# A stage function of its own for the banded attention of layer 0: two query tiles a step, the sink inside the minimum, four store buffers

## What is computed

```python
def swa_sink_attention(q, k, v, bias_table, sinks):      # 8 query heads, 2 key heads, HD = 64
    ...                                                  # each chunk of 64 sees itself and the chunk before
    s = jnp.einsum('bcqhgd,bckhd->bhgcqk', qc, kb) * ATTN_SCALE + bias
    s = jnp.where(valid[:, None, :], s, -jnp.inf)
    sink = jnp.broadcast_to(sinks..., s.shape[:-1] + (1,))
    p = jax.nn.softmax(jnp.concatenate([s, sink], axis=-1), axis=-1)[..., :WINDOW]
    o = jnp.einsum('bhgcqk,bckhd->bcqhgd', p, vb)
```

## Time and profile before

| | |
|---|---|
| median of 3 runs (2572.9 to 2577.78) | 2573.3 us |
| the profiled execution's own time | 2574.83 us |
| its span, first to last instruction | 2573.0 us |
| PE busy | 2390.8 us (93%) |
| DVE busy | 1524.9 us (59%) |
| ACT busy | 1139.8 us (44%) |
| POOL busy | 1072.9 us (42%) |
| stage B, first matmul to first matmul of the output stage | 977.91 to 1089.62 us |

### The profile page before, as it was taken

How to read it: one execution, slowest core, us unless ns; L and a number is a source line. 1 busy time by engine, 2 the same in 40 slices (tenths; PEclk the granted TensorE clock), 3 DMA queues, 4 the chain that set the end, 5 groups by cost and what they waited for, 6 DMA issues and landing times. The chain is left out here.

```text
span 2573.0 us, 46411 instructions
## 1 busy us (share of the span) xinstructions
PE 2390.8 (93%) x17864; PEld 1979.2 (77%) x17864; DVE 1524.9 (59%) x2879; ACT 1139.8 (44%) x2400; POOL 1072.9 (42%) x853
## 2 busy tenths in 40 slices
PE   5999999997999998899979999899997999998998
PEld 4777778875878877678767888788886888887887
DVE  6444665435898896756554423744223888887555
ACT  4333343333777776612133333433332666665221
POOL 6777768772000002211058877678874201100000
PEclk9999999997999999999989999999998999999999
DMA  3555434457565224657334444344433453443452
GB/s 129 174 172 176 153 124 156 142 170 161 119 144 111 62 96 140 176 190 279 130 123 164 164 115 143 112 156 160 143 99 121 156 193 133 161 157 112 160 201 82
DMA packets 220746, 376.77 MB, mean 146 GB/s; under 512 B 54980, under 2 KB 108912, under 8 KB 219504
## 3 DMA queue, kind: packets, MB, share of 16 engines
q1 hardware_dynamic: 199376, 296.21, 36.0%
q0 software_dynamic: 19792, 75.50, 9.9%
q10 hardware_dynamic: 1360, 2.10, 0.2%
HBM read 236.33 MB, written 142.90 MB: 147 GB/s over the span
## 5 line engine op out<-in xcount | busy, mean ns | idle before, releaser
L1092 PE MATMUL p_acc<-p_operands,p_w_hi 128*128 128x512 f32 x1600 | 612.0, 393 | 5.7 <-DVE p_full_out L959 5.5
L1092 PE MATMUL p_acc<-share,p_w_hi 128*128 128x512 f32 x1024 | 385.3, 397 | 12.0 <-DVE p_operands L735 5.7
L310 POOL TENSOR_TENSOR p_w_lo<-p_w_raw,p_w_hi 128x512 fp32r<-128x512 f32 x240 | 333.2, 1397 | 151.1 <-ACT p_w_hi L573 150.8
L1092 PEld LDWEIGHTS p_acc<-p_operands,p_w_hi 128*128 128x128 f32 x1600 | 302.7, 190 | 67.7 <-POOL p_w_raw L328 4.7
L1092 PE MATMUL p_acc<-share,p_w_lo 128*128 128x512 f32 x896 | 350.7, 391 | 0.0
L573 ACT ACTIVATE p_w_hi<-p_w_raw 128x512 fp32r<-128x512 f32 x252 | 156.6, 624 | 245.5 <-POOL p_w_raw L328 106.5
L1092 PE MATMUL p_acc<-share_low,p_w_hi 128*128 128x512 f32 x624 | 249.3, 400 | 12.0 <-DVE p_operands L735 6.1
L1092 PE MATMUL p_acc<-share_low,p_w_lo 128*128 128x512 f32 x624 | 245.2, 393 | 0.0
L1092 PEld LDWEIGHTS p_acc<-share,p_w_hi 128*128 128x128 f32 x1024 | 192.4, 189 | 54.0 <-DVE p_operands L735 8.5
L865 DVE SCALAR_TENSOR_TENSOR p_lo_out<-p_full_out,p_hi_out 128x512 fp32r<-128x512 f32 x116 | 122.6, 1057 | 182.5 <-ACT p_hi_out L590 182.5
L1898 DVE CUSTOM_DVE_ANT_0 c_prob<-c_logits,c_bias 128x640 f32<-128x640 f32 (+4 forms) x256 | 179.5, 739 | 65.6 <-PE c_logits L1812 49.5
(11 more groups left out here) (283 smaller groups left out, 4771.1 us busy)
## 6 DMA issues: line engine op xcount, KB each, us to landing
scr_qh<-p_hi_out SPq DMA_DIRECT2D x116, 256.0 KB, 2.5
scr_ql<-p_lo_out SPq DMA_DIRECT2D x116, 256.0 KB, 2.6
p_w_raw<-in_w_in_even POOLq DMA_DIRECT2D x26, 1024.0 KB, 7.5
scr_gt<-p_hi_out SPq DMA_DIRECT2D x128, 128.0 KB, 2.0
ready_w<-in_w_in_odd POOLq DMA_DIRECT2D x16, 1024.0 KB, 7.0
p_w_raw<-in_w_in_odd POOLq DMA_DIRECT2D x16, 1024.0 KB, 6.9
share<-scr_qh SPq DMA_DIRECT2D x28, 512.0 KB, 8.4
share<-scr_ql SPq DMA_DIRECT2D x28, 512.0 KB, 9.6
```

The source lines that it names most:

```text
L310: nc.gpsimd.tensor_tensor(w_lo[:, k, :, :], w_source(e, k), w_hi[:, k, :, :].bitcast(F32), ALU.subtract).then_inc(w_made, 1)
L1092: last = nc.tensor.matmul(bank[:, :], wt[:, k, c, :], at[k][:, c, :], start=starts and step == 0, stop=step == 3 * HK - 1, skip_group_chec ...
```

## The change

Stage B gets a function of its own, `small_attn`, and `band_attn` keeps only what stage C uses. What is different in stage B:

- A step is two query tiles of a pair of heads: 32 steps in place of 64. PE does 12 `qk` rows, 16 transposes and 16 `pv` rows a step; DVE four minima and one copy of both tiles (L2093; in a pair's first step, where 64 columns of each half are not written, two copies).
- The logits of a step take four PSUM banks of two sets; `turned` stays single, and holds both tiles.
- The sink is the starting value of the minimum, read from `keep["sink"]` for each partition. Logits and bias have 256 columns. The sink's share of the sums is added once at the end: a subtraction on DVE (L2101), an exponential on ACT (L2136), an addition on DVE.
- The column of zeros and its four memsets, and the wait of PE for them, are gone.
- There are four output buffers and four store semaphores, one for each quarter of the rows. The copy of a block waits for the store of the same quarter of the pair before. In the output stage `load_block(b)` waits for the stores of quarter b.

```diff
-        nc.gpsimd.tensor_copy(bias[:, :, NEAR], self.keep["sink"][:, :]).then_inc(masked, 1)
...
-        self.stored = [ctx.enter_context(nc.semaphore(f"{name}_stored{i}")) for i in range(2)]
+        self.stored = [ctx.enter_context(nc.semaphore(f"{name}_stored{i}")) for i in range(TILES // TPB)]
...
-                    act.wait_ge(stored[n % 2], 16 * (n // 2))
+                    act.wait_ge(stored[(n - 2) % STORES], 16 * ((n - 2) // STORES + 1))
...
+def small_attn(nc, before, keep, scr, w_dram, w_loaded, w_hi, w_lo, post, share, ready, ssq, rms):
...
+            def qk(n):
...
+                if n >= 2:
+                    pe.wait_ge(max_done, 2 * TWO * (n - 1))
+                for j, i in tiles_of(n):
...
+            def transposes(n):
+                if n >= 1:
+                    pe.wait_ge(copied, copies[n])
+                for j, i in tiles_of(n):
+                    for a in range(2):
+                        pe.wait_ge(exp_done, 2 * TWO * n + 2 * j + a + 1)
...
+            for n in range(N + 2):
+                if n < N:
+                    qk(n)
+                if 1 <= n <= N:
+                    transposes(n - 1)
+                if n >= 2:
+                    pv(n - 2)
...
+                        nc.vector.tensor_tensor_reduce(out=prob[:, n % 2, j, half, 0:cols], in0=logits[n % 2][half][:, (j + 1) * NEAR - cols:(j + 1) * NEAR],
+                                                       in1=bias[:, h, NEAR - cols:NEAR], scale=1.0, scalar=keep["sink"][:, h:h + 1],
+                                                       op0=ALU.add, op1=ALU.min, accum_out=neg_max[:, h, i:i + 1]).then_inc(max_done, 1)
...
+            for n in range(N + 1):
+                if n < N:
+                    maxima(n)
+                if n == N:
+                    dve.wait_ge(max_done, 2 * TWO * N)
+                    nc.vector.tensor_tensor(sink_exp[:, :, :], neg_max[:, :, :], keep["sink"][:, :].unsqueeze(2).to_broadcast([P, B_HEADS, TILES]), ALU.subtract).then_inc(sink_less, 1)
+                if n >= 1:
+                    leaves(n - 1)
+            dve.wait_ge(root_done, 1)
...
+            nc.vector.tensor_tensor(sums[:, :, :], sums[:, :, :], sink_exp[:, :, :], ALU.add).then_inc(summed, 1)
...
+            def output_leaves(g):
+                act.wait_ge(pv_done, 2 * (g + 1))
+                hp, r = divmod(g, STORES)
+                if hp >= 1:
+                    act.wait_ge(stored[r], 16 * hp)
+                nc.scalar.activation(o_out[:, r, :], o_ps[:, g % 2, :], ACT.Copy).then_inc(o_done, 1)
...
-                    sp.wait_ge(post.stored[1], 16 * post.heads)
+                sp.wait_ge(post.stored[b], 16 * (post.heads // 2))
```

More of the change, by code:

```diff
@@ L1597, in widen, with band_attn @@
                               self.inv_sums[:, :, t:t + 1].to_broadcast([P, self.heads, HD])).then_inc(self.widened, 1)
-def band_attn(nc, before, name, keep, scr, heads, back, q_row, k_row, group, v_dram, skew, o_row, sinks, w_dram, w_loaded, w_hi, w_lo, post, share, ready=None, ssq=None, rms=None, ahead=None):
+def band_attn(nc, before, name, keep, scr, heads, back, q_row, k_row, v_dram, skew, o_row, w_dram, w_loaded, w_hi, w_lo, post, share, ahead):
     with ExitStack() as ctx:
@@ L1696, in _ @@
         def _(sp):
[L1697 to L1704, removed]
+            for n in range(len(FIRST)):
+                first_piece(sp, n, 0)
+            for n in range(HALVES):
+                load_qk(sp, 1, n)
+                load_v(sp, 1, n)
             def store(hp, r):
@@ L1776, in _ @@
             for n in range(D // W_PART):
[L1777 removed]
+                if 2 <= n < HP:
                     load_bias(n)
@@ L1812, in qk @@
                             last = nc.tensor.matmul(logits[half][:, lo:hi], q_sb[b][x][rows, i * P:(i + 1) * P],
-                                                    k_sb[kb][y][rows, tile * P:tile * P + hi - lo], start=n == 0, stop=n == 2)
+                                                    k_sb[b][y][rows, tile * P:tile * P + hi - lo], start=n == 0, stop=n == 2)
                 last.then_inc(qk_done, 1)
@@ L1854, in pv @@
                     for half in range(2):
-                        v = v_sb[:, hp % 2, half, i - w + 1 + t, :] if ready is None else v_sb[:, k_set(hp), i - w + 1 + t, :]
-                        last = nc.tensor.matmul(o_ps[half * HD:(half + 1) * HD, group, at:at + P], v,
+                        v = v_sb[:, hp % 2, half, i - w + 1 + t, :]
+                        last = nc.tensor.matmul(o_ps[half * HD:(half + 1) * HD, at:at + P], v,
                                                 prob_t[:, s % 2, t, half, :], start=t == 0, stop=t == w - 1)
                 last.then_inc(pv_done, 1)
-            if sinks:
-                pe.wait_ge(zero_set, 2 * SETS)
             for s in range(PAIRS + 2):
@@ L1871, in _ @@
         def _(dve):
-            links = [0]
-            def link(ins):
-                links[0] += 1
-                ins.then_inc(rms_done, 1)
-                dve.wait_ge(rms_done, links[0])
-            if ssq is not None:
-                nc.vector.tensor_scalar(mean[:, :, :], ssq[:, :, :], 1.0 / P, EPS, ALU.mult, ALU.add).then_inc(mean_done, 1)
-            if sinks:
-                for s in range(SETS):
-                    for s_ps in logits:
-                        nc.vector.memset(s_ps[:, end(s):end(s) + 1], 0.0).then_inc(zero_set, 1)
-                dve.wait_ge(zero_set, 2 * SETS)
             def maximum(s, half):
@@ L1891, in maximum @@
                 j, n = (2 * s + half) % 4, width(s) * P
-                if i == 0 and half == 0 and ready is None:
+                if i == 0 and half == 0:
                     dve.wait_ge(bias_set, hp + 1)
@@ L1914, in _ @@
                     main_leaves(s - 1)
-            if ssq is not None:
-                dve.wait_ge(root_done, 1)
-                link(nc.vector.reciprocal(rms[:, :, :], root[:, :, :]))
-                sharpen(nc, link, rms[:, :, :], mean[:, :, :], root[:, :, :])
             dve.wait_ge(exp_done, 2 * PAIRS)
@@ L2179, in trunk @@
                     post = OutputReady(nc, mid, "post0", scr, B_HEADS, [low[:, 2 * x:2 * x + 2, :] for x in range(3)] + [high[:, :, :]])
[L2180 to L2181 removed]
+                    stage = small_attn(nc, stage, keep, scr, src["w_out_even"][0], w_loaded[1], w_hi, w_lo, post, share, small, ssq, rms)
                 with mid:
@@ L2191, in trunk @@
             post = OutputReady(nc, mid, "post1", scr, C_HEADS, [whole[:, 2 * x:2 * x + 2, :] for x in range(4)])
-            stage = band_attn(nc, stage, "c", keep, scr, C_HEADS, 4, 0, C_W, 1, scr["v1"], scr["skew_c"], 0, False,
-                              src["w_out_odd"][0], w_loaded[3], w_hi, w_lo, post, [whole[:, x, :] for x in range(8)], ahead=band_ahead)
+            stage = band_attn(nc, stage, "c", keep, scr, C_HEADS, 4, 0, C_W, scr["v1"], scr["skew_c"], 0,
+                              src["w_out_odd"][0], w_loaded[3], w_hi, w_lo, post, [whole[:, x, :] for x in range(8)], band_ahead)
             stage = output(nc, stage, "o1", keep, scr, scr["x1"], w_hi, w_lo, None, out, src["final_g"], post)
```

298 lines of the change are left out of this document (220 added, 78 removed).

## The result

The changed kernel takes 2561.7 us (median of five), 0.9947 of the kernel before on the same chip, 95% interval 0.9932 to 0.9961: 13.6 us less by the ratio (2559.7 us), 11.6 by the two medians, where 9.3 were forecast. A second set of runs gave 0.9953 (0.9940 to 0.9966): 12.1 us less by the ratio (2561.2 us), 11.1 by the medians. The profiled execution took 2567.35 us with a span of 2565.5 and is the longest of its five; what it is longer by lies outside stage B (first experiment). So stage B is read by its own stretch, from its first matmul to the output stage's first: 111.74 us before, 98.25 after, 100.33 in the second run's profile.

What follows compares the result with a forecast made beforehand. Stage B was taken to be bound by a loop in which DVE and PE wait for each other. Steps -9.6, start -0.3 and end +0.6 gave -9.3 us, so 2564.0 us, range 2560.3 to 2568.5.

Steps and rivals of the forecast that it cites:

- The rule of the step: Stage B's loop: two steps take PE's 3.03 us plus DVE's 2.86, 5.89 together, so 2.94 a step against 3.25.
- PE's side: Stage B, from DVE's copy through transposes, `pv` and logits to the next minimum: 3.03 us, against 1.87 for one tile.
- DVE's side: Stage B, minima to copy: four minima 1.64 us and one copy 1.22, 2.86 against 2.78 before.
- the half-sum: Stage B's step as half of PE's and DVE's sides added together, 2.94 us in the forecast.
- Sixteen transposes: Stage B on PE, start of transposes to `pv`: old 0.45 us plus 0.36 for eight more, 0.81.
- logits to minimum: Stage B, start of logits on PE to DVE's minimum: old 0.78 us plus 0.36 for six more rows, 1.14.
- Rival 1: DVE alone sets stage B's step at 2.86 us: sum -11.8, 2561.5 us; this rival or more, 19%.
- Rivals 2 to 4: PE bound, 3.25 a step, 2573.6 us, 9%; query loads or stores late, 2568, 13%; lower PE clock, 2598.1, 4%.
- The cold start: Stage B's first steps at clock 0.50: counted at the same gain per step, 0.9 us either way.
- The end: Stage B's last first minimum to the reciprocal's end: 7.85 us against 7.27, 0.6 lost, 0.5 either way.
- The store buffers: Stage B's end: four buffers keep SP's stores behind the eight loads covered, cost nothing; SP late by 4.5 us otherwise.
- a sign of being wrong: At stage B's end, SP ending after POOL would show the forecast wrong.

Runs made afterwards that it cites:

- first experiment: The changed kernel timed and profiled once more with nothing edited: 2563.4 us, ratio 0.9953 to the kernel before.
- the constant: The changed kernel with the minima of a step started from a constant in place of the sink in memory: 2558.6 us, ratio 0.9935.
- more on PE: The changed kernel with the first key tile's product with the values done twice in each step: 2565.8 us, ratio 0.9968.
- experiment 9: The changed kernel with DVE's wait for the transposes put ahead of its wait for the logits, as before the change: 2562.0 us, ratio 0.9957.
- experiments 3 and 10: The changed kernel with one query tile a step, 2575.9 us, ratio 1.0004; the kernel before with stage B's minima started from memory, 2578.3 us, ratio 1.0008.
- experiments 7 and 9: The changed kernel with a memset more on DVE each step, 2560.6 us; with the first key tile's product done twice on PE, 2565.8 us; and experiment 9.
- experiment 4: The changed kernel with two buffers for the raw weights that POOL works on beside stage B: 2559.0 us, ratio 0.9940.
- experiment 6: The changed kernel with two buffers for the stored outputs in place of four: 2564.8 us, ratio 0.9961.
- experiment 8: The kernel before with DVE's wait for the logits put first ahead of the minimum, in stages B and C: 2567.0 us, ratio 0.9975.

## Why the prediction was right and wrong

**The rule of the step was right for the changed kernel.** Two steps together take PE's side, from copy to minimum, and DVE's side, from minimum to copy. With both sides read in one run that is bound to come out (2.74 + 2.84 = 5.58, and two steps take 5.59); nor was it a test that the loop before agreed with its window to 0.01. The test is whether a side stays as it is when the other is edited, and it does: with 2.74 carried over, the half-sum gives 2.67 for the constant (2.67 measured), 3.01 for more on PE (3.01) and 2.84 for the old order of waits (2.845).

**The step that failed is PE's side, 3.03 us.** It is 2.74, so a step is 0.15 us shorter than forecast, 4.3 us over 29 intervals. Two of its terms were too large. Sixteen transposes were put at 0.45 + 0.36 = 0.81 and take 0.64 to the next group. And logits to minimum was put at 0.78 + 0.36 = 1.14 and is 1.02. Of the last 0.12 us, 0.107 come from the order of the two waits ahead of the minimum (experiment 9), which the changed lines show and the forecast did not cost at all. `pv` was put at 1.03 and is 1.03.

The transposes were too dear because the old rows hold a wait for a third engine, which the account of the loop had left out. ACT in the kernel before, PE's weight loads before, and the same loads now:

```profile
1078.24 0.49 ACT L1929 ACTIVATE b_prob<-b_prob,b_neg_max 128x257 f32<-128x257 f32 x1
```

```profile
1078.70 0.38 PEld L1833 LDWEIGHTS b_turned<-keep_ident,b_prob 64*128 64x128 f32 x8
```

```profile
1020.25 0.58 PEld L2039 LDWEIGHTS b_turned<-keep_ident,b_prob 64*128 64x128 f32 x16 [0.32 <-DVE b_prob_t L2093]
```

ACT's exponential of the second head ends at 1078.73, when the transposes have begun. In the single loads of the trace, the second head's first one starts 0.14 us after that end, at every step late in the stage, and so the eight pause in the middle: their pairs start 0.06 us apart, but 0.12 where the second head begins. With two tiles a step the exponentials are done in time but for a pair's first step, all pairs start 0.06 apart, and eight more loads cost 0.20 us of span, not 0.36. The forecast had the pause of 0.06 us three times, once in the 0.45 and twice in the 0.36; that is its error of 0.17. So in the kernel before, the loop ran through ACT too, by 0.06 us. This accounts for the half of its price that a dearer minimum cost there (experiments 3 and 10); no run edited ACT itself.

**DVE's side held** (2.86 forecast; four minima 0.405 apart and a copy of 1.22 make 2.84), with the price of the start from memory taken from stage A. Rival 1 came near by the time, since DVE alone needs 2.76 a step (the shorter of the two alternating steps; the next minimum then starts 0.08 before the copy ends, so that the copy costs DVE itself 1.14, and the forecast's fixed part of 0.155 is right for the copy's span alone), but it doesn't set the step (experiments 7 and 9). Rivals 2 to 4 didn't come: PE is less busy, no DMA ends a wait of PE or DVE in the loop, and the granted clock stays 1.00.

**The cold start** was counted at the ordinary gain with 0.9 us either way; the first two intervals give 2.1 us more than that, and the first minimum, which now waits for the logits of two tiles, takes 1.0 back. Why the two intervals gain that much was not tested.

**The end** was put 0.6 us longer and is 1.6 and 3.0. The sum to the reciprocal, 7.85, is right to the hundredth when POOL is idle (experiment 4), by luck at that: the forecast gave it 0.5 us either way. I had not asked where POOL's weight work would be in a shorter stage. It ends 92.7 us after the stage's first matmul (84.7 before), and the stage's end came 13 us earlier, onto it. Its operations last as long as before (1.03 and 2.37 us for each of eight parts); what grew is the time between them, in which the next load is issued and lands, and why is open. The Trainium skill (SBUF — State Buffer, SBUF: two separate sides) says that an operation of VectorE with two inputs in SBUF and one of GpSimd that reads SBUF shut each other out for a whole instruction. The rows agree: L79 and L80, with two inputs, end 0.07 and 0.08 us after POOL's subtraction, and the reciprocal beside it, with one, takes 0.55 as without it. That POOL waits in its turn, no row here shows.

**The store buffers** at nothing: right for four; with two the end is 2.3 to 3.7 us later (experiment 6), as the account of SP's queue said. It is close: SP's last issue ends 0.13 us after POOL in the first profile, which the forecast had named as a sign of being wrong, and 1.04 before it in the second. The output stage begins 1.02 us after POOL's end in both, so SP sets nothing there.

Sum for the first profile: -9.3, then -4.3 (the 29 intervals), -2.1, +1.0 and +1.0 (the end) make -13.7, with 13.9 found (13.5 in the stage and 0.4 ahead of it). The last three nearly cancel, by luck. In the second profile the stage gains 11.4 us, and most of the difference is the end.

## What to carry to other kernels

When two engines hand work back and forth with two steps under way, a step takes half of what both sides need, and a delay on either side costs half its length, as long as no third engine is on the loop. Before a group is doubled, look inside it for a wait: a pause in the old group must not be multiplied with its rows. Look at the order of waits ahead of an instruction on such a loop: the one that comes last in time should be the first written (here 0.11 us each). And when a stage is made shorter, ask what work beside it ended comfortably before, and now ends with it.

## What the runs showed that was not expected

- Of two waits ahead of the minimum, the one written second stands in the trace as an instruction of its own, and the minimum starts 0.105 us after it; the one written first the minimum itself carries. From logits to minimum it is 0.773 us with the logits' wait second and 0.664 with it first, with nothing else changed (experiment 8).
- A DVE operation of 128x64 took 2.38 us in place of 0.22 beside a POOL operation of 2.34 us.
- A minimum of 256 columns with its start from memory starts 60 ns later behind another one (405 against 345), as stage A's rows of 640 columns said (884 ns long against 822).
